# Attention jobs: the score scale in the queries' norm weights, both maxima in one reduction, results copied by ScalarE

## The reference, cut to what matters

```python
qa = rmsnorm_2(qa.reshape(...), qk_g[0])        # 8 heads of 64; likewise ka by qk_g[1]
qb = rmsnorm_2(qb.reshape(...), qk_g[2])        # 4 heads x 2 maps of 64; likewise kb by qk_g[3]
# both with a rotary embedding for the 256 tokens
def gqa_attend(q, k, v):
    s = einsum('bqhgd,bkhd->bhgqk', q * HEAD_DIM ** -0.5, k)
    return einsum('bhgqk,bkhd->bqhgd', softmax(s), v)
def diff_attend(q, k, v, lam):
    s = einsum('bqhmd,bkhmd->bhmqk', q * HEAD_DIM ** -0.5, k)
    p = softmax(s)
    return einsum('bhqk,bkhe->bqhe', p[:, :, 0] - lam * p[:, :, 1], v)
```

## Time and profile before

| What | us |
|---|---|
| median of 3 runs (lowest, highest) | 3076.93 (3074.41, 3081.26) |
| the profiled execution | 3082.64 |
| its span, first to last instruction | 3080.8 |
| layer 0's attention jobs, from the first scores to the last values | about 1446 to 1548.7 |
| layer 1's attention jobs | about 2693.6 to 2755 |

### The profile page before, as it was taken

The page is one execution under the profiler, slowest core; times in us unless marked ns, Lnnn a source line. Parts: engine busy times, 40 slices in busy tenths (PEclk is TensorE's granted clock), DMA queues, the critical chain, the costliest instruction groups (busy, mean ns, idle before and its releaser), DMA issues.

```text
span 3080.8 us, 56010 instructions
## 1 busy us (share of the span) xinstructions
PE 2916.9 (95%) x24149; PEld 2382.8 (77%) x24149; DVE 1505.7 (49%) x2220; ACT 1025.7 (33%) x1499; POOL 303.6 (10%) x397
## 2 busy tenths in 40 slices
PE   8999878999999899999899999999999998989999
PEld 8877565777677599876578878888788887669999
DVE  6644232323223466672853444445544456386666
ACT  5421113222222344533632332222322225264543
POOL 0242000000000000241100000000100004310000
PEclk9998888999999999999999999999999999999999
DMA  6566779999989845310012232222222222104552
GB/s 226 183 243 223 306 301 396 420 364 368 391 364 380 343 165 191 110 69 28 1 55 109 96 123 96 96 96 96 70 96 95 96 96 93 44 15 185 215 188 83
DMA packets 77072, 547.91 MB, mean 178 GB/s; under 512 B 8384, under 2 KB 10432, under 8 KB 11056
## 3 DMA queue, kind: packets, MB, share of 16 engines
q1 hardware_dynamic: 76000, 540.05, 45.3%
q0 software_dynamic: 848, 4.57, 0.4%
HBM read 637.91 MB, written 1.05 MB: 207 GB/s over the span
## 4 chain that ended last, share of the span: by engine, by line
PE 86%; DVE 5%; DMA 4%; ACT 2%; POOL 1%; issue 1%; DVEq 0%; SPq 0%; POOLq 0%; ACTq 0%
PE bank L787 56%; PE bank L1170 10%; DMA ring<-slabs 4%; PE bank L1520 2%; PE bank L851 2%; DVE tiny L2882 1%; PE bank L885 1%; PE bank L893 1%; PE bank L889 1%; PE bank L1372 1%; PE bank L1376 1%; PE bank L1379 1%; PE bank L986 1%; PE bank L1689 1%; PE bank L1697 1%
## 5 line engine op out<-in xcount | busy, mean ns | idle before, releaser
L787 PE MATMUL bank<-hhi,whi 128*128 128x256 f32 (+1 forms) x1280 | 431.3, 337 | 0.6 <-ACT wk L2072 0.4
L787 PE MATMUL bank<-hlo,whi 128*128 128x256 f32 (+1 forms) x1280 | 430.4, 336 | 0.0
L787 PE MATMUL bank<-hhi,wlo 128*128 128x256 f32 (+1 forms) x1280 | 429.2, 335 | 0.0
L2254 DVE TENSOR_TENSOR wlo<-ring,whi 128x2048 fp32r<-128x2048 f32 x132 | 298.9, 2288 | 206.2 <-ACT whi L1721 200.6
L787 PE MATMUL bank<-fhl,whi 128*128 128x256 f32 (+1 forms) x1408 | 344.5, 336 | 0.0
L1721 ACT ACTIVATE whi<-ring 128x2048 fp32r<-128x2048 f32 x132 | 252.3, 1914 | 209.8 <-PE bank L787 209.8
L1170 PE MATMUL bank<-ring,wk 128*32 128x256 f32 x4064 | 257.1, 395 | 27.6 <-DMA ring<-slabs 14.3
L787 PEld LDWEIGHTS bank<-fhl,whi 128*128 128x128 f32 x1408 | 239.9, 188 | 32.0
L787 PEld LDWEIGHTS bank<-hhi,whi 128*128 128x128 f32 x1280 | 240.4, 188 | 29.8 <-issue 1.7
L787 PEld LDWEIGHTS bank<-hlo,whi 128*128 128x128 f32 x1280 | 241.1, 188 | 26.8
L787 PEld LDWEIGHTS bank<-hhi,wlo 128*128 128x128 f32 x1280 | 240.2, 188 | 26.3
(11 more groups left out here) (526 smaller groups left out, 5579.0 us busy)
## 6 DMA issues: line engine op xcount, KB each, us to landing
ring<-slabs SPq DMA_DIRECT2D x542, 1024.0 KB
wk<-slabs SPq DMA_DIRECT2D x45, 1024.0 KB, 12.7
ac<-slabs SPq DMA_DIRECT2D x16, 1024.0 KB, 12.0
wk<-mixp POOLq DMA_DIRECT2D x1, 1040.0 KB, 7.3
xt<-xT SPq DMA_DIRECT2D x1, 1024.0 KB, 6.9
xt<-ctxT POOLq DMA_DIRECT2D x1, 1024.0 KB, 7.2
out<-xt SPq DMA_DIRECT2D x4, 256.0 KB, 2.4
cst<-maskc POOLq DMA_DIRECT2D x1, 960.0 KB, 9.0
```

Of the source, the lines that this page charges most:

```text
L787: last = pe.matmul(o, a, b, start=k == 0, stop=k == len(pairs) - 1)
L2254: tt_(wlo_of(n), slab(n), whi_of(rel).bitcast(F32), ALU.subtract).then_inc(sem("wlo"), 1)
```

## The change

The scale of the scores, 64 to the power -0.5, no longer enters at the maxima and at the exponential: once for each layer VectorE multiplies the two query columns of `qkg` by it. `maxima` becomes one reduction over both banks of the pair, which waits for both scores; so that one instruction can name two banks, the eight banks are one PSUM tensor. In `scale`, kind "b", the second map is multiplied by its factor and minus lambda in one tensor_scalar with two scalars, and the sum takes the first map times its factor. `result` moves from VectorE to ScalarE, between `exps(n + 1)` and the copies of `turns_of(n)`.

```diff
-        bank = [ctx.enter_context(nc.psum_tensor(f"bank{i}", [P, 512], F32)) for i in range(8)]
+        psum = ctx.enter_context(nc.psum_tensor("bank", [P, 8 * 512], F32))
+        bank = [psum[:, 512 * i:512 * i + 512] for i in range(8)]
...
                         act.activation(PR[n % 2][m][:, k0:T2], bank[c][:, k0:T2], ACT.Exp, bias=NM[:, c:c + 1],
-                                       scale=HD ** -0.5, accum_out=RSUM[:, c:c + 1]).then_inc(sem("ex"), 1)
+                                       accum_out=RSUM[:, c:c + 1]).then_inc(sem("ex"), 1)
+
+                def result(n):
+                    kind, j, q = js[n]
+                    act.wait_ge(sem("pv"), j0 + n + 1)
+                    act.activation(QK[:, j if kind == "a" else 5 + j, q * P:(q + 1) * P], bank[6 + n % 2][:, 0:P], ACT.Copy
+                                   ).then_inc(sem("pvc"), 1)
...
+                    if n:
+                        result(n - 1)
                     kt0 = 0 if js[n][2] < 2 else 2
                     for m in range(2 if js[n][0] == "a" else 1):
...
+                result(len(js) - 1)
                 act.wait_ge(sem("pvc"), j0 + len(js))
...
+                qg = pc("qkg", 4 * l, 4)[:, 0:4:2]
+                then(ts_(qg, qg, HD ** -0.5, None, ALU.mult))
...
-                    for m in range(2):
-                        c = 2 * (n % 2) + m
-                        dve.wait_ge(sem("sc"), 2 * (j0 + n) + m + 1)
-                        ins = dve.tensor_reduce(NM[:, c:c + 1], bank[c][:, k0:T2], AX_X, ALU.max, negate=True)
-                    then(ins)
-                    c = slice(2 * (n % 2), 2 * (n % 2) + 2)
-                    ts_(NM[:, c], NM[:, c], HD ** -0.5, None, ALU.mult).then_inc(sem("nmx"), 1)
+                    c = 2 * (n % 2)
+                    both = psum[:, 512 * c:512 * c + 1024].rearrange("p (m k) -> p m k", m=2)
+                    dve.wait_ge(sem("sc"), 2 * (j0 + n) + 2)
+                    dve.tensor_reduce(NM[:, c:c + 2], both[:, :, k0:T2], AX_X, ALU.max, negate=True
+                                      ).then_inc(sem("nmx"), 1)
...
-                        tt_(RREC[:, c + 1:c + 2], RREC[:, c + 1:c + 2], NLAM, ALU.mult)
-                        then(ts_(p0, p0, RREC[:, c:c + 1], None, ALU.mult))
-                        ins = stt(p0, p1, RREC[:, c + 1:c + 2], p0, ALU.mult, ALU.add)
+                        then(ts_(p1, p1, RREC[:, c + 1:c + 2], NLAM, ALU.mult, ALU.mult))
+                        ins = stt(p0, p0, RREC[:, c:c + 1], p1, ALU.mult, ALU.add)
                     ins.then_inc(sem("pn"), 1)
-
-                def result(n):
-                    kind, j, q = js[n]
-                    dve.wait_ge(sem("pv"), j0 + n + 1)
-                    dve.tensor_copy(QK[:, j if kind == "a" else 5 + j, q * P:(q + 1) * P], bank[6 + n % 2][:, 0:P]
-                                    ).then_inc(sem("pvc"), 1)
...
-                    if n:
-                        result(n - 1)
...
-                result(len(js) - 1)
```

## The result

The changed kernel takes 3052.98 us, the median of 4 runs (3048.72 to 3054.36); the kernel before took 3079.1 us beside it (4 runs, 3074.41 to 3082.51). The ratio is 0.9921, with a 95% interval from 0.9905 to 0.9937: 24 us faster, between 19 and 29. Forecast were 13.3 us and a time of 3063.6. The side was right, the size was half of what came.

The account below looks back on a forecast made before the run. TensorE, busy 95% of the span, bounds the kernel; VectorE savings count only where it waits in the attention stages. Terms 3.8 + 7.0 + 2.2 + 0.3 = 13.3 us off the 3076.93 median give 3063.6, range 3057 to 3071.

Parts of the forecast that it names:

- Layer 0's first half: Layer 0's attention jobs of kind "a": shorter chain to the scaling TensorE waits for; -2.2 us, bounds 0 and -5.2.
- 0.28 of each 0.65: Layer 0's first half: gain taken from each of TensorE's eight waits for L2895, 5.2 us in all.
- rival D: Layer 0's second half: waits go and the clock stays up, up to 3.6 us more gain, 3058 to 3061; chance 0.10.
- Layer 0's second half: Eight wide and eight narrow jobs of kind "b": from 45.50 to 38.5 us, -7.0, bounds -3.2 and -10.2.
- Layer 1's second half: Eight wide jobs of kind "b": from 25.50 to 21.7 us, -3.8.
- TensorE's 2.76 us a job: Wide job of kind "b": TensorE's transposes 0.60, scores 1.06 and values 1.10 together.
- Layer 1's first half: Opening wait of 2.2 us, for two reductions and L2885 ahead of the first exponential, becomes shorter; -0.3 us.
- The prices: Estimated instruction times: merged reduction 1.21 us, result copy on ScalarE 0.28, tensor_scalar with two pointers 0.48.
- the prediction's slope: VectorE reductions: 1.04 ns per added element, from 681 ns at 512 and 414 at 256; merger saves 0.07 us a wide job.
- A: Half the gain: two-pointer scaling 0.27 us dearer, or merged reduction as much as two; 3066 to 3070 us; chance 0.14.
- B: No change: ScalarE's result copies overrun their 0.37 us cover and delay its later work; 3077 us; chance 0.10.
- C: Slower: two-bank reduction at half pace, 1.1 us longer in a wide job; 3086 to 3091 us; chance 0.04.

Follow-up runs that it names:

- copy_later: Kernel before, with VectorE making each result copy one job later; 3067.77 us, ratio 0.9964.
- split_pn: Changed kernel, with VectorE signalling after each of its two scalings in jobs of kind "a"; 3054.01 us, ratio 0.9930.
- copy_only: Kernel before, with only the result copies moved from VectorE to ScalarE; 3060.81 us, ratio 0.9950.
- no_copy_move: Changed kernel, with the result copies back on VectorE behind the scaling; 3065.65 us, ratio 0.9966.
- scale_only: Kernel before, with only the score scale moved into the norm weights, so L2885 goes; 3066.08 us, ratio 0.9972.
- fill_pe: Kernel before, with unneeded matmuls added in TensorE's waits in layer 0's second half; 3076.50 us, ratio 0.9991.
- two_reduces: Changed kernel, with one reduction for each bank in place of the merged one; 3058.16 us, ratio 0.9943.
- copy_twice: Changed kernel, with a second ScalarE copy of the same size ahead of each result copy; 3056.35 us, ratio 0.9936.
- result_late: Changed kernel, with ScalarE's result copy put behind the copies of the transposes; 3054.86 us, ratio 0.9927.
- after_again: Changed kernel run and profiled once more, nothing altered; 3054.45 us, ratio 0.9919.
- copy_no_wait: Changed kernel, with a VectorE instruction of the copy's size added in the copy's old place, waiting for nothing; 3061.15 us, ratio 0.9943.

## Why the prediction was half of it

**Two steps failed: the term for layer 0's first half, -2.2, was sized too small, and the clock was left out of the sum.**

**Layer 0's first half** measured -6.2. The mechanism was named ("the reductions no longer start behind a copy that waits for the values") and the size was guessed: 0.28 of each 0.65 that TensorE waited for the scaling. Of these 5.2 us, 4.1 are gone. copy_later, which removes only the wait, takes 4.4 us off this half at an unchanged clock. The far end that the prediction itself gave, all of the 5.2, was the better reading: TensorE's next wait, for ScalarE, took little of the gain back (3.4 us now, 3.1 before); ScalarE's own wait ahead of those copies fell from 23.7 to 5.2 us. Up to 1.7 of the 6.2 are the clock.

**The clock.** 10.2 us at 1.2 GHz are gone from layer 0's stage. That is worth 5.1 us at most, if TensorE had work all through, and 3.0 by split_pn's price; in the sum it stood at nothing. The prediction kept it apart, as rival D with a chance of 0.10, and for the second half alone. It was not another way for things to go but a second term that came with the first one, in both halves. It goes with changes of the same waits, but what exactly decides over a dip is not shown: the one behind the opening vanished with L2885 alone, the other one where both the copy's wait and the rest had gone (copy_only and no_copy_move each keep it; scale_only and split_pn's profile have half of it), or where fill_pe filled the half.

**Layer 0's second half:** forecast -7.0, to 38.5; measured -8.2, to 37.4. That the size is nearly right is luck. 6.8 us at 1.2 GHz had cost up to 3.4 us, which leave 4.8 to 6.2 for the waits, less than forecast. A row of the trace before, which the prediction does not show, has the wait that counted: 7.9 us of the transposes for the scaling of kind "b", of which 4.8 are gone.

**Layer 1's second half:** -4.5 for -3.8. TensorE's 2.76 us a job was a sum of three pieces of a chain, as if each began at the end of the one before; from scores to scores it is 2.59. Nor did VectorE's 2.91 us with branch_low slow the jobs shown above. **Layer 1's first half:** -0.4 for -0.3.

**The prices** were good where a row of the same line lay near: 1.22 for 1.21, 0.284 for 0.28. The tensor_scalar with two pointers took 0.55 for 0.48, on an engine that now waits 12.9 us for scores in layer 0's stage. The Trainium skill ("ScalarE: Activation LUTs", rules for kernel authors) gives `relu`, `max`, `min`, `add` and `mul` to VectorE and not to ScalarE. A copy is not in that list; the prediction took it in. Here the same copy takes 0.28 us on either engine (the 0.29 that the prediction estimated for ScalarE is a little more than that, not no more), and to have it on ScalarE takes 11.1 us off the stages, because what the copy waits for then holds no reduction. The measurement decides. For the merged reduction the estimate of 1.19 us, worked out from the Trainium skill ("VectorE: DVE Perf Modes", section on the TRN2 errata), comes near the 1.22. What the merger saves, 0.8 us of the stages by two_reduces, is too little to tell that estimate from the prediction's slope.

**The rivals.** A needed a dearer reduction or scaling; only the scaling was dearer, by a quarter of what A assumed (0.07 of 0.27). B is out by copy_twice and result_late, C by the 1.22. D took place, beside a gain in the waits that was larger than forecast.

**The sum.** Without the clock's 3.0 to 5.1 us the stages gave 14.2 to 16.3 us, against 13.3 forecast: near it, because the first half was put too low and the second too high. Behind layer 1's stage some 1.0 us is gone in both profiles of the changed kernel (325.9 to 324.9); what did that is open. That makes 20.3, inside the measured 19 to 29, and 3056.6 us if taken off the 3076.93.

The remaining 4 us of the ratio come from no part of the edit that was tried. Where they lie can be read from the mean granted clock of each run: twice what it lacks to 1.00, times the span, is the time at 1.2 GHz. It makes 182 us at 1.2 GHz in the mean of the 62 runs of the kernel before that stand beside the experiments, and 161 in the ten of the changed kernel (after and after_again): 21 us less, of which the stages' profiles show 10.2. Among the runs of one kernel a us more at 1.2 GHz goes with 0.33 us (before) and 0.38 us (changed) more time, so the other 11 make some 4 us. They do not come with the stages as they now are: in four kernels whose stages show no dip in layer 0 either (copy_no_wait, two_reduces, copy_twice, result_late; 18 runs) the mean is 169 us, and their ratios are 17 to 23 us. Whether the ten runs had less by chance was not shown.

## What to carry to other kernels

Ask of each instruction in an in-order queue not only how long it is but what it waits for, and what stands behind it that doesn't need this: one small copy that waited for TensorE cost 11 us where an instruction of nearly its size without the wait cost 1.3. Making the copy one job later on the same engine gave 8.4 us with an edit of three lines; moving it to another engine gave 11.1. Where the granted clock of a stretch is under 1.00 and TensorE waits there, count the clock as part of the wait's price from the start, and not as a separate event: here 10.2 us at 1.2 GHz went with the waits.

## What was not expected of the hardware

An instruction of 0.17 us on two columns decided over a clock dip: with L2885 all five profiles have 3.4 us at 1.2 GHz behind the opening of layer 0's stage, without it none of nine. The wait of TensorE's that stands ahead of it, for the first exponentials, is 2.20 us with L2885 and 1.99 without (before and scale_only). Both dips stand at the same places in the two profiles of the instructions before, and in fill_pe the dip of the second half went away when TensorE got work of no use. Two VectorE instructions that differ only in a second scalar by pointer and its multiplication, L2898 before and L2907 after, differ by 0.07 us (0.48 and 0.55). That the second scalar is the cause is not shown: the scalings of kind "a", with one scalar and the same shape, took 0.53 and 0.54 us before and 0.59 and 0.60 after.
